# Rotation angles in the pooling sums' buffer from step 4 on, the first norm's weights loaded there, and the first step's rows turned by VectorE

## The reference

```python
def swiglu(x, w13, w2):
    gate, up = jnp.split(x @ w13, 2, axis=-1)      # w13: 1024 x 5632
    return (jax.nn.silu(gate) * up) @ w2           # w2: 2816 x 1024

def rope(x, positions):
    ang = positions.astype(jnp.float32)[..., None] * inv_freq
    cos, sin = jnp.cos(ang), jnp.sin(ang)          # used by the mixing part only
    ...

for l in range(DEPTH):
    x = layer_norm(ALPHA * x + 0.5 * swiglu(x, ffn1_w13[l], ffn1_w2[l]), ln_g[l, 0], ln_b[l, 0])
    ...                                            # mixing part, memory part
    x = layer_norm(ALPHA * x + 0.5 * swiglu(x, ffn2_w13[l], ffn2_w2[l]), ln_g[l, 3], ln_b[l, 3])
```

## Time and profile before

| | us |
|---|---|
| Median of 3 runs | 1094.37 |
| Lowest and highest of them | 1094.14 and 1094.89 |
| The profiled execution's own time | 1095.91 |
| Its span, from the first instruction to the last | 1094.1 |
| PE busy in the span | 1082.2 |
| DVE busy | 847.9 |
| ACT busy | 534.8 |
| POOL busy | 80.4 |

### The profile page before, as it was taken

The page is one execution under the profiler, slowest core; times in us unless marked ns, Lnnn a source line. Parts: engine busy times, 40 slices in busy tenths (PEclk is TensorE's granted clock), DMA queues, the critical chain, the costliest instruction groups (busy, mean ns, idle before and its releaser), DMA issues.

```text
span 1094.1 us, 16586 instructions
## 1 busy us (share of the span) xinstructions
PE 1082.2 (99%) x5720; PEld 933.6 (85%) x5720; DVE 847.9 (77%) x1450; ACT 534.8 (49%) x731; POOL 80.4 (7%) x120
## 2 busy tenths in 40 slices
PE   9999999999999999999999999999999999999997
PEld 7888887999899888888888888889999988888885
DVE  5888887797866788778687887878977667887885
ACT  5545444566454554444454444445664645444442
POOL 0260000140100100000010000001401000000000
PEclk9999999999999999999999999999999999999999
DMA  8675756354564475665657556554546556556551
GB/s 301 197 213 186 222 184 236 111 161 168 190 214 141 153 233 178 219 189 175 212 184 226 177 182 219 173 196 122 168 152 205 179 170 196 169 192 213 173 189 58
DMA packets 156803, 203.18 MB, mean 186 GB/s; under 512 B 12656, under 2 KB 137840, under 8 KB 156752
## 3 DMA queue, kind: packets, MB, share of 16 engines
q1 hardware_dynamic: 153552, 193.25, 55.1%
q0 software_dynamic: 2912, 8.92, 2.8%
q10 hardware_dynamic: 288, 0.33, 0.1%
HBM read 201.41 MB, written 1.05 MB: 185 GB/s over the span
## 4 chain that ended last, share of the span: by engine, by line
PE 90%; DVE 4%; DMA 2%; issue 2%; SPq 1%; ACT 1%; DVEq 0%; POOL 0%; POOLq 0%; ACTq 0%
PE ps L591 87%; DVE hidden_T L1467 2%; DMA raw<-in_ffn_w 2%; PE ps L674 2%; DVE w_lo L1410 1%; SPq L540 1%; DMA raw<-in_mem_wkv 1%; DVE ev L1453 0%; PE ps L834 0%; DMA cst<-in_constants 0%; ACT ev L1203 0%; DVE tmp L1527 0%; PE ps L1069 0%; DVE x L1516 0%; PE ps L922 0%
## 5 line engine op out<-in xcount | busy, mean ns | idle before, releaser
L1161 ACT CAST w_hi<-raw 128x1024 fp32r<-128x1024 f32 (+1 forms) x247 | 255.7, 1044 | 214.2 <-DMA raw<-in_ffn_w 98.1
L1410 DVE TENSOR_TENSOR w_lo<-raw,w_hi 128x1024 fp32r<-128x1024 f32 (+1 forms) x247 | 295.9, 1222 | 82.7 <-ACT w_hi L1161 80.8
L591 PE MATMUL ps<-w_hi,xT 128*128 128x512 f32 (+1 forms) x912 | 287.3, 389 | 0.5 <-DVE xT L1443 0.5
L591 PEld LDWEIGHTS ps<-w_hi,xT 128*128 128x128 f32 x912 | 171.0, 188 | 35.8 <-DVE xT L1443 0.7
L591 PE MATMUL ps<-w_hi,mixT 128*128 128x512 f32 x688 | 198.1, 390 | 0.1
L1161 ACT CAST v_flat<-raw 128x1024 fp32r<-128x1024 f32 (+1 forms) x114 | 118.7, 1045 | 141.1 <-DMA raw<-in_ffn_w 77.8
L1467 DVE STREAM_TRANSPOSE hidden_T<-ev 32x128 f32<-32x128 f32 x576 | 174.5, 303 | 8.6
L591 PE MATMUL ps<-v_flat,xT 128*128 128x512 f32 (+1 forms) x660 | 177.2, 389 | 0.0
L591 PE MATMUL ps<-w_lo,xT 128*128 128x512 f32 (+1 forms) x456 | 175.3, 388 | 0.0
L591 PEld LDWEIGHTS ps<-w_hi,mixT 128*128 128x128 f32 x688 | 128.7, 188 | 26.8 <-issue 0.5
L591 PEld LDWEIGHTS ps<-v_flat,xT 128*128 128x128 f32 x660 | 123.7, 188 | 25.3 <-DVE cqp L1410 0.2
(11 more groups left out here) (168 smaller groups left out, 1223.2 us busy)
## 6 DMA issues: line engine op xcount, KB each, us to landing
raw<-in_ffn_w SPq DMA_DIRECT2D x352, 256.0 KB, 3.7
raw<-in_ffn_w SPq DMA_DIRECT2D x88, 512.0 KB, 5.2
raw<-in_mem_wkv SPq DMA_DIRECT2D x32, 512.0 KB, 4.8
raw<-in_w_out SPq DMA_DIRECT2D x16, 512.0 KB, 4.6
raw<-in_mem_wq SPq DMA_DIRECT2D x16, 512.0 KB, 5.8
raw<-in_mem_wo SPq DMA_DIRECT2D x16, 512.0 KB, 4.6
gb<-in_ln_g POOLq DMA_DIRECT2D x8, 512.0 KB, 4.4
gb<-in_ln_b POOLq DMA_DIRECT2D x8, 512.0 KB, 6.2
```

Of the source, the lines that this page charges most:

```text
L591: return nc.tensor.matmul(dst, stand, move, start=start, stop=stop, skip_group_check=True)
L1161: nc.scalar.copy(slot_hi[slot[n]][:, 0:size], raw[:, n % RAW, 0:size]).then_inc(hi_done, 1)
L1410: nc.vector.tensor_tensor(slot_lo[slot[n]][:, s], raw[:, n % RAW, s], slot_hi[slot[n]][:, s].bitcast(F32), ALU.subtract).then_inc(lo_done, 1)
```

## The change

It has three edits. First, DVE turns step 0 of e = 3, 4 and 7 too (`by_blocks` is true for e + s > 0), and PE's 4 transposes there go. Step 0 of e = 0 stays on PE. Second, the positions and angles live in `poolM` (the buffer of the pooling sums, seen as `pool_flat`), and POOL begins them after PE has used unit 23 of e = 0 in place of unit 11, that is in up(4) in place of up(2). Third, `load_gains(0)` stands right behind the issue of the positions' loads, ahead of the angles; the wait for the tables moves behind the first norm.

```diff
-    BLOCK_TURNED = FS - 2
+    BLOCK_TURNED = FS - 1
...
-            marks += [UNIT_] * 2 + ([[("hidden", e, 0)]] if s == 1 else []) + (turned(2) + turned(3) if e == 0 and s == 1 else [])
+            marks += [UNIT_] * 2 + ([[("hidden", e, 0)]] if e == 0 and s == 1 else []) + (turned(2) + turned(3) if e == 0 and s == 1 else [])
...
-        def by_blocks(s):
+        def by_blocks(e, s):
-            return 0 < s < FS - 1
+            return e + s > 0 and s < FS - 1
...
+        pool_flat = poolM[:, :, :].rearrange("p t s -> p (t s)")
...
-                        if j == 1 and s == 1:
+                        if j == 1 and s == 1 and e == 0:
                             turn_hidden(0)
...
-                ahead_to(u + 7) if e == 0 else ahead(("hidden", e, 0))
+                ahead_to(u + 7) if e == 0 else ahead(("unit", u + 5))
...
-                        angle = gb[:, 0, i * TB * HALF:(i + 1) * TB * HALF].rearrange("p (b c) -> p b c", b=TB)
+                        angle = pool_flat[:, i * TB * HALF:(i + 1) * TB * HALF].rearrange("p (b c) -> p b c", b=TB)
...
-            pool.wait_ge(pe_done, done["unit", plan["ffn", 0, 0]["units"] + 11])
+            pool.wait_ge(pe_done, done["unit", plan["ffn", 0, 0]["units"] + 23])
             for b in range(TB):
-                pool.dma_start(gb[:, 1, b:b + 1].bitcast(I32),
+                place = 5 * TB * HALF + b
+                pool.dma_start(pool_flat[:, place:place + 1].bitcast(I32),
                                a["positions"][0, b * P:(b + 1) * P].rearrange("(p o) -> p o", o=1)).then_inc(pos_landed, 16)
+            load_gains(0)
             rope_angles()
...
-            pool.wait_ge(tables_done, 1)
-            load_gains(0)
             for l in range(L):
                 norm(4 * l)
+                if l == 0:
+                    pool.wait_ge(tables_done, 1)
```

## The result

The changed kernel takes 1101.55 us (median of 6 runs, 1100.33 to 1104.51) against 1094.46 us for the kernel before (6 runs, 1094.14 to 1095.41): a ratio of 1.0069, with a 95% interval of 1.0059 to 1.0079. That is 7.1 us slower, where 3.1 us was forecast, and above the range, which ended at 1099.2.

A forecast was written before the change was run, and what follows sets the result against it. PE was taken as the bound, with e = 0 paced by its weight supply. Edit 1's +0.72, edit 2's 0 and edit 3's +2.4 summed to +3.1 us on 1094.37, so 1097.5 us, range 1094.9 to 1099.2.

The forecast's parts named there:

- +0.54, +0.62, -0.44, sum +0.72: Edit 1 at down(0) of e = 3, 4 and 7: losses of 0.54 and 0.62 us, gain of 0.44, together +0.72.
- the cover of 0.4 us: At down(1) of e = 3: remainder ready at 410.69, PE there at 411.11, so the later refill costs nothing.
- The term was 2.4 us: Edit 3 at step 4 of e = 0: norm weights beside the critical weight load delay it by 2.4 us.
- 3.2 us is the upper bound: Edit 3's largest price, from loads landing after 6.7 us beside the norm loads at 560 us, 3.5 without.
- three quarters of the price: Edit 3: critical loads issued at the same time are partly served first, so 2.4 us of 3.2 is taken.
- the chain loses in full what it loses at step 4: End of e = 0: no slack wins the delay back, so +2.4 us, 1.2 at step 4, the rest at step 10.
- the wait at step 10: PE's transposes of step 10 of e = 0 wait some 2.5 us in place of 1.3.
- No engine waits for either. I cost it at nothing: Edit 2, positions and angles 12 units later in e = 0: no cost, within 0.3 us either way.
- The hidden norm weights: Rival: the norm weights in e = 0 cost nothing, only edit 1's +0.7 remains, 1095.1 us; chance 0.11.
- The spared queue: Rival: e = 3, 4 and 7 keep most of 1.5 us, chain loses 2.4 or less, 1095.6 us; chance 0.08.
- The fast case: Rival: without norm weights at 166 the late load at 174.08 lands sooner, 2.8 us won, 1091.6; chance 0.07.
- The worse case: Rival: three parts miss step 1's cover (+1.5), step 4's unit pays 3.2, in all +5.4, 1099.8 us; chance 0.10.

The follow-up runs named there:

- e1: Edit 1 alone against the kernel before, with positions, angles and norm weights issued where they were: 1095.72 us, ratio 1.0011.
- e7: Edit 1 alone, with DVE forming the remainder of the turned rows ahead of some splits, against the kernel before: 1094.43 us, ratio 0.9994.
- e3: Edit 3 alone against the kernel before: positions, angles and small loads at unit 11, norm weights after unit 23; 1096.94 us, ratio 1.0023.
- e9: The whole change with only one of two norm loads at unit 23, the second at unit 38: 1098.15 us, ratio 1.0033 against the kernel before.
- e6: Edit 3 alone with the norm weights three units later, after unit 26, against the kernel before: 1094.63 us, ratio 0.9996.
- e2: Edit 2 alone against the kernel before, norm weights still behind the tables: 1094.69 us, ratio 1.0003.
- e5: The whole change, but POOL issues the small loads only after unit 32 of e = 0: 1099.64 us, ratio 1.0045 against the kernel before.
- e4: Edits 2 and 3 as in the change, without edit 1, against the kernel before: 1100.52 us, ratio 1.0055.
- e10: The whole change with the norm weights issued ahead of the positions: 1099.38 us, ratio 1.0045 against the kernel before.

## Why the prediction was wrong

**Bound and method: right.** PE at 98 to 99%, e = 0 paced by its supply, e = 3, 4 and 7 by DVE's queue: every loss lies in one of these two, though not always in the step that was named.

**Edit 1: right.** Forecast +0.54, +0.62, -0.44, sum +0.72. Measured in the change +0.51, +0.51, -0.21, sum +0.8; in e1, by the same marks, +0.55, +0.79, -0.31, sum +1.0, and +1.3 by the medians. A further 0.13 and 0.16 us are lost at down(1) of e = 7, without a wait that the profile lists. The series works as told. DVE's timeline of the changed kernel in e = 3, for the earlier trace rows:

```profile
390.04 0.69 DVE L1454 TENSOR_TENSOR ev<-ps,ev 128x512 f32<-128x512 f32 x1 [0.90 <-ACT ev L1204]
390.77 5.05 DVE L1468 STREAM_TRANSPOSE hidden_T<-ev 32x128 f32<-32x128 f32 x16
395.85 1.23 DVE L1411 TENSOR_TENSOR w_lo<-raw,w_hi 128x1024 fp32r<-128x1024 f32 x1
...
400.39 0.68 DVE L1474 TENSOR_TENSOR mixT<-hidden_T,mixT 128x512 fp32r<-128x512 f32 x1
```

From the product's start to the remainder's end it is 11.03 us; the prediction's 5.81 + 4.55 + 0.68 is 11.04. At down(1) of e = 3 the change has no wait, so the cover of 0.4 us held, and e7 showed how thin it is. The Trainium skill's rule ("VectorE: DVE Perf Modes", section "Rules for kernel authors") to leave transposes of this size to TensorE agrees with the sum, though not with e = 7: sixteen stream transposes take 5.05 us of DVE here, and the PE transposes they replace 0.49 us of PE.

**Edit 3: right mechanism, wrong size.** The critical unit of step 4 was named, and so were its issue at 77.8 and the path from its landing over rounding, split and product to down(4). The term was 2.4 us, with 3.2 as the upper bound; it measured 4.35. The first step that failed is "beside the same two norm loads at 560 us, six weight loads took 6.7 us to land, against 3.5 without them: 3.2 us is the upper bound". Around 560 us SP's queue was empty when the norm weights were issued (its last load before was of 548), and six loads shared what came after. At 78 us the unit ahead of the critical one had just been issued, and the critical one shared the DMA engines with that, with both norm loads, and with those behind it. So the rows at 560 are of another situation and were no bound; that this difference is the reason is argued, no run tried it. I took three quarters of the price on the argument that an issue at the same time is served in part ahead; the table says otherwise. Issued 1.5 us ahead of the critical unit (e3) the price is 2.2 us, and from 1 us ahead to 0.3 behind it 3.3 to 4.35. (e3 also lacks the positions' loads and POOL's angles in that stretch, so that its lower price is the phase's isn't shown by itself.) What decides within that microsecond the runs leave open: the executions differ too little and too irregularly. Half the bytes gave 2.7 us (e9). That it is the meeting, and not the megabyte, e6 shows with 0.

The Trainium skill ("DMA: Bandwidth & Descriptors", section "Issuing engines are not separate DMA queues") has transfers of different engines interleaved on the same 16 DMA engines. The trace agrees: SP's loads of 256 KB from 78 to 89 us land after 7.5 us in the median, and the critical one after 8.86.

**Where it goes: half right.** I wrote that the chain loses in full what it loses at step 4. By the medians it is nearly so, e3 costing 2.5 us in all with 2.2 at step 4; its profiled execution alone, 0.85 at the end, would not have shown it. But the place was told wrong: the wait at step 10 stayed at 1.2 us in place of growing to 2.5, since PE had paid already. The first unit of step 5 that needed a split waited 2.37 us, which is not in the prediction at all: behind a late load, not only the product but the splits queued behind it on DVE are late, and DVE's transposes lie between.

**Edit 2: a failed step.** "No engine waits for either. I cost it at nothing" is the second step that failed. Alone that holds (e2, +0.3). Its small loads are 8 us of issues, which I had put near 97 to 105 and whose meeting with the critical loads of step 5 I did not look up. In the change they start at 95.25, step 5's critical loads go out from 98.2 because edit 3 has made them late, and they land after 6.6 and 6.4 us where e2's took 3.2 and 4.0: +1.70 us in the profile, 2.0 to 2.4 against the undisturbed steps of the other kernels, about 2 by e5. It isn't enough that they meet, as e9 shows; what in the phase decides stays open here too. With edit 3's larger price it makes the 3.3 us between e4 and the sum of e2 and e3. Edits of which each was costed against the trace of before were not costed against each other.

**The sum.** 1.28 + 4.35 + 1.70 at steps 2 to 5, less about 1 us won back up to the end of e = 0, is 6.36; with 0.81 and 0.13 for edit 1 it is 7.3. Which of the terms the 1 us belongs to, the traces don't tell: at step 10 the kernels without a meeting stand between 1.7 us ahead of before (e2) and 0.3 behind it (e7).

**The rivals.** The hidden norm weights fell (8.86 us). The spared queue fell (the waits at down(0) of e = 3 and 4). The fast case fell: without norm weights at 166 the load of the chain there still took 5.13 us. PE waited 1.2, 0.7 and 1.1 us at step 10 in the change, e3 and e4, all without norm weights at 166, and less than 0.2 us in e1, which has them there: the wait that was to go isn't theirs. The worse case, 1099.8, was nearest in size, and half of its reason was wrong: it had the cover of step 1 gone, which held. Its other half, that the unit of step 4 pays more, came true (4.35 us where it took 3.2), and the meeting at step 5 it didn't have.

**What stays open.** How the microsecond of phase sets the price between 3.3 and 4.35 us. Each row of the table is one execution, and the time from issue to product varies by some 0.6 us without any norm weights (6.9 in e1, 7.58 before), so the differences within that group are not much more than this. The changed kernel's own runs spread over 4 us, where before's spread over 1.3; that fits a price that hangs on a microsecond of phase, but no run here shows it. By which rule the DMA engines serve the meeting transfers, no run shows either.

## What to carry to other kernels

A stage that lives from its loads has a critical unit in each step. Look up when it is issued and when it lands, and put foreign transfers behind its landing; here three units (7.7 us) later turned 2.5 us into 0. An edit that costs nothing against the old trace must be costed again against the trace as the other edits shift it, its small DMAs too. And a bound from another place in the trace is one only if the queue ahead of the transfer looks the same there.

## What was not expected of the hardware

- A load of 256 KB of SP, issued beside POOL's two loads of 512 KB, landed after 8.2 to 8.9 us in place of 3.9 to 4.5, twice its time, while the norm loads in the change took 6.7 and 8.5 us. SP's load of the unit ahead, issued at 78.18, 0.4 us before the first norm load, still took 3.5.
- Sixteen small loads of 0.5 to 128 KB, 0.5 MB in all, stretched the loads of step 5 from 3.2 and 4.0 us (e2) to 6.6 and 6.4 in the change. In e9, with the first of them 0.3 us ahead of the critical unit in place of 4.5, that unit's loads took 3.6 and 4.0.
- POOL's angles of 128 x 64 took mostly 0.37 us each in the change, but now and then 1.2 us: 14.0 us for all in the change and 14.1 in e4, 18.5 before, 18.2 in e2, 18.1 in e10. It goes with what DVE does. Before, the 12 of them that ran beside a split or another TENSOR_TENSOR of DVE took 0.78 us in the mean and up to 1.22, the 11 beside its block transposes 0.35, no more than the 3 beside an idle DVE. In e10, these took over 1 us each while DVE was at its splits from 94.09 to 98.9:

```profile
95.64 1.04 POOL L1821 TENSOR_TENSOR poolM<-poolM 128x64 f32<-128x64 f32 x1
96.76 1.22 POOL L1820 TENSOR_SCALAR poolM<-poolM 128x64 f32<-128x64 f32 x1
98.07 1.04 POOL L1821 TENSOR_TENSOR poolM<-poolM 128x64 f32<-128x64 f32 x1
```

In the change DVE waited 5.77 us for the late load in the middle of the angles, and only 5 of them ran beside a TENSOR_TENSOR. That this is why POOL was faster is read from the traces; no experiment tried it alone.
